# The first token tile runs ahead in both MLPs; low weight halves go into the ring slots; ScalarE casts the input's high halves

## The reference, cut to what matters

```python
h = x
for layer in range(2):                 # layer 0: differential attention, layer 1: block attention
    mix = attention(h)                 # w_in, scores, softmax, w_out
    h = layer_norm(ALPHA * h + mix, ln1_g[layer], ln1_b[layer])
    h = layer_norm(ALPHA * h + square(relu(h @ w_up[layer])) @ w_down[layer], ln2_g[layer], ln2_b[layer])
u = modulate(rmsnorm(h))               # third block: token mixer (retention and latent attention)
h = h + gate * token_mixer(u)          # w_in_2 is 1024 x 6848, and six more matrices
h = h + gate * hier_moe(modulate(rmsnorm(h)))   # 32 experts, 2 per token
out = rmsnorm(h)
```

## Time and profile before

| | us |
|---|---|
| median of three runs | 1192.47 (1191.81 to 1195.05) |
| profiled execution | 1190.7 |
| its span | 1188.9 |
| TensorE busy | 1118.6 (94%) |
| VectorE busy | 699.5 (59%) |
| ScalarE busy | 556.3 (47%) |

### The profile page before, as it was taken

The page is one execution under the profiler, slowest core; times in us unless marked ns, Lnnn a source line. Parts: engine busy times, 40 slices in busy tenths (PEclk is TensorE's granted clock), DMA queues, the critical chain, the costliest instruction groups (busy, mean ns, idle before and its releaser), DMA issues. The chain is left out here.

```text
span 1188.9 us, 17973 instructions
## 1 busy us (share of the span) xinstructions
PE 1118.6 (94%) x7231; PEld 898.8 (76%) x7231; DVE 699.5 (59%) x1041; ACT 556.3 (47%) x953; POOL 52.4 (4%) x94
## 2 busy tenths in 40 slices
PE   7998899999999999999998999999999999889676
PEld 5987688888789987888887878988887866546333
DVE  3487867778766667778778626745456643312112
ACT  4567556556545646555655424345543322213112
POOL 5000000010000000010000000000000000000000
PEclk9999999999999999999998999999999989979988
DMA  9943378888755333888873652455647799999995
GB/s 273 290 168 104 107 224 295 292 280 292 244 163 191 108 117 130 321 293 275 285 262 100 137 177 72 142 206 180 209 139 262 280 374 369 389 398 386 417 416 225
DMA packets 126510, 285.17 MB, mean 240 GB/s; under 512 B 12222, under 2 KB 72891, under 8 KB 118369
## 3 DMA queue, kind: packets, MB, share of 16 engines
q1 hardware_dynamic: 116512, 249.29, 59.9%
q0 software_dynamic: 9920, 34.80, 9.1%
HBM read 281.87 MB, written 2.20 MB: 239 GB/s over the span
## 5 line engine op out<-in xcount | busy, mean ns | idle before, releaser
L2000 DVE TENSOR_TENSOR w_lo<-ring,w_hi 128x1024 fp32r<-128x1024 f32 (+1 forms) x272 | 320.3, 1212 | 101.1 <-ACT w_hi L1507 91.7
L1507 ACT ACTIVATE w_hi<-ring 128x1024 fp32r<-128x1024 f32 (+1 forms) x272 | 277.0, 1047 | 102.8 <-PE acc L680 77.2
L678 PE MATMUL acc<-w_hi,x_two 128*128 128x512 f32 (+2 forms) x320 | 128.5, 402 | 5.3 <-DVE x_two L1985 4.1
L680 PE MATMUL acc<-w_hi,x_two 128*128 128x512 f32 (+2 forms) x320 | 123.4, 386 | 0.0
L679 PE MATMUL acc<-w_lo,x_two 128*128 128x512 f32 (+2 forms) x320 | 123.3, 385 | 0.0
L678 PE MATMUL pp<-x_two,w_hi 128*128 128x256 f32 x384 | 112.5, 293 | 0.0
L679 PE MATMUL pp<-x_two,w_hi 128*128 128x256 f32 x384 | 108.5, 283 | 0.0
L680 PE MATMUL pp<-x_two,w_lo 128*128 128x256 f32 x384 | 108.5, 283 | 0.0
L678 PE MATMUL acc<-w_hi,hid_hi 128*128 128x512 f32 x256 | 99.8, 390 | 0.0
L680 PE MATMUL acc<-w_hi,hid_lo 128*128 128x512 f32 x256 | 99.6, 389 | 0.0
L679 PE MATMUL acc<-w_lo,hid_hi 128*128 128x512 f32 x256 | 99.6, 389 | 0.0
(11 more groups left out here) (397 smaller groups left out, 2135.4 us busy)
## 6 DMA issues: line engine op xcount, KB each, us to landing
ring<-in_w_up_dram SPq DMA_DIRECT2D x32, 1024.0 KB, 5.7
ring<-in_w_down_dram SPq DMA_DIRECT2D x32, 1024.0 KB, 6.6
exp_ring<-in_w_dram SPq DMA_DIRECT2D x32, 1024.0 KB, 11.3
stage<-in_w_ada_dram POOLq DMA_DIRECT2D x48, 512.0 KB, 6.2
ring<-in_w_in_dram SPq DMA_DIRECT2D x24, 1024.0 KB, 5.3
ring<-in_w_in_a_dram SPq DMA_DIRECT2D x12, 1024.0 KB, 14.2
mod<-in_w_dram SPq DMA_DIRECT2D x19, 512.0 KB, 12.9
ring<-in_w_kv_shared_dram SPq DMA_DIRECT2D x8, 1024.0 KB, 6.2
```

Of the source, the lines that this page charges most:

```text
L678: pe.matmul(out, lhs[0], rhs[0], start=start, stop=False)
L680: return pe.matmul(out, lhs[1], rhs[0], start=False, stop=stop)
L1507: act.activation(shaped(high_half(b, k), raw), raw, ACT.Copy).then_inc(S["hi_ready"], 1)
L2000: dve.tensor_tensor(shaped(low_half(b, k), raw), raw, shaped(high_half(b, k), raw), ALU.subtract).then_inc(S["lo_ready"], 1)
```

## The change

1. *Ring and high slots.* `w_lo` goes; `w_hi` has eight halves. For blocks 12 to 99 the low half is written over the raw values in its ring slot, and SP reloads a slot only when TensorE has used the block (`half_used`) instead of when its low half is ready. Other blocks use the upper half of `w_hi` for their lows, as deep as before.
2. *Input.* In all 16 parts ScalarE writes `x_hi` itself, one activation of 128 x 512 behind its four scaled pieces; VectorE only subtracts.
3. *MLP start.* The fillers ahead of each turn go (two remain after the first). Up blocks 0 and 1 run by tile: block 0 on tile 0 (by input halves), the turn of tile 1, block 1 on tile 0, block 0 on tile 1, block 1 on tile 1, then down block 0. Block 0 sums in `acc` banks 0 and 1; the other pairs swap `pp` and `tp`. For one tile the low product has 128 columns and the high product 2 x 128.
4. *MLP end.* Down 14 leaves the second half of tile 1 for later: 18 products, then down 15 on tile 0 (12), then the remaining 6 of down 14 and 12 of down 15.
5. *By tile elsewhere.* `tile_first_out` runs blocks 0 and 1 on tile 0 before tile 1, and the turn of tile 1 stands after block 0's twelve products instead of after six.
6. *Norms.* VectorE normalises tile 0 first, takes the rest of tile 1's sum, and splits parts of tile 0 between; ScalarE casts the first high half of block 1 before the root of tile 1 and the second one after it.
7. *Expert stage.* In the last quad five fillers stand between the w1 product and the wait for w3.

```diff
-HIGHS = 4
+HIGHS = 8
-LOWS = 4
+def in_place(b):
+    return B_ATT[0] + 12 <= b < B_RQK
...
@@ low_half, load
+            if in_place(b):
+                return raw_half(b, k, low_ring)
+            return w_hi[:, HIGHS // 2 + high_slot(b, k), :]
...
+                    if in_place(old):
+                        sp.wait_ge(S["half_used"], half_index(old, 1) + 1)
...
@@ tile_first_out
-                for j in range(4):
-                    if j % 2 == 0:
-                        half_ready(b, j // 2)
-                    part(0, j, 0)
-                    if j == 1:
+                for i in range(2):
+                    for j in range(4):
+                        if j % 2 == 0:
+                            half_ready(b + i, j // 2)
+                        part(i, j, 0)
+                    if i == 0:
                         turn()
                 pe.wait_ge(S["x_split"], base + 3)
-                for j in range(4):
-                    last = part(0, j, 1)
...
@@ TensorE, mlp
+                def up_tile(v, c, k, q):
+                    tok = slice(q * 128, (q + 1) * 128)
+                    sums = up_banks(v)[:, c, :].rearrange("p (a n) -> p a n", a=2)[:, :, tok]
+                    if k == 0 and q == 0:
+                        half_ready(b + v, c)
+                    for kt in range(4 * k, 4 * k + 4):
+                        hi, lo = w_parts(b + v, c, slice(128 * kt, 128 * kt + 128))
+                        if kt:
+                            pe.matmul(sums[:, 0, :], lo, x_hi[:, kt, tok], start=False, stop=False)
+                        last = pe.matmul(sums, hi, x_two[:, :, kt, tok], start=(kt == 0), stop=(kt == KT - 1))
...
+                norm_tile(2 * layer, 0)
+                busy(2)
+                for k in range(2):
+                    pe.wait_ge(S["x_split"], base + 1 + k)
+                    for c in range(2):
+                        up_tile(0, c, k, 0)
+                norm_tile(2 * layer, 1)
+                for c in range(2):
+                    for k in range(2):
+                        up_tile(1, c, k, 0)
+                for k in range(2):
+                    pe.wait_ge(S["x_split"], base + 3 + k)
+                    for c in range(2):
+                        up_tile(0, c, k, 1)
+                for c in range(2):
+                    for k in range(2):
+                        up_tile(1, c, k, 1)
+                down(0)
...
+                for v in range(PAIRS - 2, PAIRS):
+                    pe.wait_ge(S["hid_ready"], PAIRS * layer + v + 1)
+                    for f in range(2):
+                        half_ready(b + min(2 * v + 2, 31), f)
+                    last_parts(v, 0, (0, 1))
+                    if v == PAIRS - 2:
+                        last_parts(v, 1, (0,))
+                last_parts(PAIRS - 2, 1, (1,))
+                last_parts(PAIRS - 1, 1, (0, 1))
...
@@ expert stage, last quad
+                    if s + 1 == QUADS:
+                        busy(5, turn_bank)
...
@@ ScalarE, to_input and norm_input
+                    act.activation(x_hi[:, 4 * half:4 * half + 4, q * 128:(q + 1) * 128], x_f[:, n % 2, :, :],
+                                   ACT.Copy).then_inc(S["xs_high"], 1)
...
                 norm_root(i, 0)
+                scaled(0, 1)
+                high_part(b + 1, 0)
                 norm_root(i, 1)
+                high_part(b + 1, 1)
                 scaled(0, 1)
+                if i != 1:
+                    high(b + 2)
...
@@ VectorE, split_part and layer_norm
-                dve.wait_ge(S["tp_done"], turns_done(g))
+                dve.wait_ge(S["xs_high"], n + 1)
-                link(dve.tensor_copy(x_hi[:, at[0], at[1]], x_f[:, n % 2, :, :]))
...
+                normalise(0)
+                sum_part(i, b, 1, 0)
+                half_sum(i, b, 1, 1)
+                split_input(1)
+                link(half_stats(1, 1))
+                tile_stat(1)
+                split_input(1)
+                normalise(1)
+                low((B_MLP[0], B_ATT[1], B_MLP[1])[i] + 1)
+                split_input(2)
+                if i != 1:
+                    low((B_MLP[0], B_ATT[1], B_MLP[1])[i] + 2)
```

More of the change, by code:

```diff
@@ L689, in w_parts @@
             def w_parts(b, k, cols):
-                return high_half(b, k)[:, cols], low_half(b, k)[:, cols]
+                low = low_half(b, k)
+                if len(low.shape) == 3:
+                    assert cols.stop - cols.start == 128
+                    return high_half(b, k)[:, cols], low[:, cols.start // 128, :]
+                return high_half(b, k)[:, cols], low[:, cols]
             def arrive(b):
@@ L975, in mlp @@
                 inputs[0] += 4
-                def before(j):
-                    if j < 2:
-                        pe.wait_ge(S["x_split"], base + 3 + j)
                 def up(v):
[L983 to L986, removed]
+                    pe.wait_ge(S["sum_done"], PAIRS * layer + v - 1)
+                    pairs_out(b + 2 * v - 1, up_banks(v))
+                def up_tile(v, c, k, q):
[8 more added lines that the diff above has]
+                        last = pe.matmul(sums, hi, x_two[:, :, kt, tok], start=(kt == 0), stop=(kt == KT - 1))
+                        if kt == 0:
+                            pe.matmul(sums[:, 0, :], lo, x_hi[:, kt, tok], start=False, stop=False)
+                    if k == 1 and q == 1:
+                        last.then_inc(S["half_used"], 1)
                 def down_part(v, j, q):
@@ L1007, in mlp @@
+                for k in range(2):
[6 more added lines that the diff above has]
+                down(0)
+                for v in range(1, PAIRS - 2):
                     up(v + 1)
-                    if v == 0:
-                        pe.wait_ge(S["ln_stat"], 4 * layer + 2)
@@ L1010, in mlp, with last_parts @@
                     down(v)
[L1011 to L1015, removed]
+                up(PAIRS - 1)
+                def last_parts(v, q, halves):
+                    for half in halves:
                         for f in range(2):
-                            last = down_part(PAIRS - 1, 2 * f + half, q)
+                            last = down_part(v, 2 * f + half, q)
@@ L1671, in mlp @@
                         .then_inc(S["rest_ready"], 1)
-                    high(b + 2 * v + 2 - (v > 0) if v < PAIRS - 1 else b + 31)
+                    if v:
+                        high(b + 2 * v + 1)
                     act.wait_ge(S["sum_done"], j + 1)
@@ L1956, in _ @@
             inputs = [0]
-            input_groups = [g + i for g in SHIFTED_AT for i in range(4)]
             plain = [0]
@@ L1996, in low_part @@
                 dve.wait_ge(S["hi_ready"], x + 1)
-                if x >= LOWS:
-                    dve.wait_ge(S["half_used"], x - LOWS + 1)
+                if x >= HIGHS // 2 and not in_place(b):
+                    dve.wait_ge(S["half_used"], x - HIGHS // 2 + 1)
                 raw = raw_half(b, k)
```

87 lines of the change are left out of this document (39 added, 48 removed).

## The result

The changed kernel takes 1202.27 us (median of 18 runs, 1192.34 to 1207.35), the kernel before 1188.01 us in 18 runs on the same chip (1181.80 to 1195.05). The ratio is 1.0113, 95% interval 1.0094 to 1.0132: 13.4 us slower. The forecast was 1196.0, range 1190 to 1209. The direction was right and the range held it; the forecast is 6.3 us short.

The account below looks back on a forecast made before the run. TensorE, busy 94% of the span, was taken as the bound, the change being decided at its breaks. +1.8 - 1.3 + 5.7 - 2.65 = +3.6 us on 1190.7 gives 1194.3; with 1.8 for the median, 1196.0, range 1190 to 1209.

Parts of the forecast that it names:

- Input and MLP start: At both MLP starts, the first down product comes 0.9 us later with a pair at 0.23 us: +1.8 in all.
- End of the MLPs: Ahead of the last down block TensorE idles 1.2 us; price and gain both about zero.
- The second norm: At the norm of i = 1, block 2 starts at 339.1 instead of 340.40: -1.3 us.
- Norm ahead of the third block: TensorE idles 5.6 us awaiting block 97's halves, then runs at low clock: +5.7 us, ends 3.55 and 7.
- What follows: Behind the third block's start, loads of blocks 100 to 105 and latents shift by the same as the products.
- Ring and depth: Loads waiting for TensorE's use of a block instead of its low half make nothing wait; worth nothing.
- Last quad: Five fillers in a 4.9 us wait keep 2.4 GHz; the 64 products cost 3.7 instead of 6.35 us: -2.65.
- small products dear: Rival at MLP starts: small products cost more than columns and load, pair up to 0.347, 1209.5 us; chance 0.17.
- the clock holding: Rival ahead of the third block: no low clock behind the idle stretch, 2.1 us less, 1194; chance 0.12.

Follow-up runs that it names:

- g1_wide: The changed kernel with each low product of an MLP's first two half blocks taking 256 columns instead of 128: 1201.6 us, ratio 1.0121.
- e3_ring: The changed kernel with low halves in ring slots only up to block 95, so loads 100 to 103 wait for low halves again: 1197.3 us, ratio 1.0085.
- f1_late: The changed kernel with block 105's halves cast behind the latents' copies and first four query projections (VectorE: their rotations): 1191.7 us, ratio 1.0037.
- e1_early: The changed kernel with block 97's high and low halves cast ahead of the second tile's input, not behind the whole input: 1195.1 us, ratio 1.0052.
- g2_noplace: The changed kernel with block 97's halves early and 105's late, but no low halves in ring slots and four high halves: 1201.8 us, ratio 1.0121.
- f4_before_busy: The kernel before with only the last quad's five fillers added: 1185.0 us, ratio 0.9970.
- g3_again: The changed kernel without any edit, run and profiled a second time: 1201.7 us, ratio 1.0109 against the kernel before.
- g4_before_late: The kernel before with the last quad's five fillers and block 105's halves cast late: 1184.7 us, ratio 0.9975.
- e4_both: The changed kernel with block 97's halves early and the old ring rule from block 96 on: 1190.3 us, ratio 1.0010.

## Why the prediction was right in sign and short in size

- *Input and MLP start* (+0.9 each, a pair at 0.23): right. 0.23 measured, 21.76 against 20.74 us, +1.0. g1_wide shows that columns don't set the price, as the prediction said; that the load of the weights does, it leaves likely but not shown. By the 81 ns of the Trainium skill (TensorE: Matmul & The Clock Gate, Back-to-back issue gap) a pair at 0.20 would have come out, an estimate from that figure and the 0.12 of a 256-column product. The trace doesn't agree for these products: 0.11 is left for the one of 128 columns, and the measurement decides.
- *End of the MLPs* (1.2 us idle, price nothing): right, 1.08 idle; the next norm's first product is no later.
- *The second norm* (first product 326.56, block 2 at 339.1): 326.57 and 339.16.
- *Norm ahead of the third block* (5.6 us idle to 652.1, low clock behind it, +5.7 at block 98): 5.55, to 652.17, at 0.50; +5.6.
- "What follows (loads of blocks 100 to 105, latents) waits for the same products and shifts by the same": **this step failed**. It is the one sentence of that part without a row. Block 98 is 5.6 us late, the latents' first product 10.3, the next attention 11.2. It treated the loads as tied to the products already; before, they were tied to the low halves, which ran ahead of the products. The first projection load stood 1.6 us *ahead* of block 98's start (652.67 against 654.25); in after it goes out 4.0 us *behind* it (663.90 against 659.86), since it waits for its end. The new order lets 5.6 us pass, the new ring rule adds 5.6, and the slack that 105's cast had in before (0.50 us) didn't cover it. How far the rule is at fault, e3_ring shows: with the old rule and the new order the 4.86 us are 0.63. f1_late takes the second loss away alone, 6.4 us of the third block, e1_early the first, 6.5; together 14.2.
- *Ring and depth* ("nothing waits"; a wait could only show inside an MLP): right in the MLPs, wrong in the third block, the same gap in the argument: the loads there aren't of the MLP's kind, and nine issues follow each other. What the rule and the depth are good for was not seen either: without both the new order costs 17 us more (g2_noplace).
- *Last quad* (-2.65): right, -3.6 with an interval of 1.3 to 5.9 (f4_before_busy), -3.2 in the last quad of after; the products take 3.6 us in place of 6.3.

The sum: forecast +3.6. The terms that it has, as measured, give the same: 1.2, 5.6 and -3.2. What is missing is the term that it put at nothing, 5.6 us more in the third block. With it, it is +1.2 for the layers up to 621 us (+1.0 at the first MLP's start; in the first profile of after 1.2 us of chance in the first attention hide it: one stretch there, 103.55 to 117.20, takes 13.65 us, and 14.87 in before and in g3_again), +11.2 for the third block, -3.2 for the last quad: +9.2. The medians, against which the chance in one profile doesn't count, say +13.4, 11.2 to 15.7 by the interval. Some 4 us are therefore not placed (2 to 6.5). They may be a matter of how often the fall of the clock told below happens: the mean granted clock of after's executions has a median of 0.969, that of its profiled one is 0.972. No run shows it.

None of the rivals was this one. The nearest rules, small products dear and the clock holding, are both refuted (0.23; 0.50). That the range held the result is luck: its upper end, 1209, came from small products being dear.

## What to carry to other kernels

When a buffer's release moves from "converted" to "used", list every load behind it in the queue up to the last one that any engine waits for in its program order, and look at how early each went out before: here nine issues of 11.7 us stood between the release and the load that mattered, and the slack behind it was 0.50 us. A cast of a late block placed ahead of short urgent copies is a trap that costs nothing until the load is late; moved behind them it gave 6.4 us of the third block here and nothing where the load was early. And an idle stretch ahead of a block is best removed where the waiting engine has a hole: 97's two casts fit in ScalarE's wait for tile 1, and both moves together beat both kernels (1184.8 against 1188.2). But the kernel before with the fillers alone does as well (1185.0), so that all the rest of the change, mended, is worth nothing that these runs can tell.

## What was not expected of the hardware

Some 220 us behind the third attention's transposes, in the router's products, the clock falls with TensorE busy all along. It does so in most profiles, not in all; the same 20 us there in before and in g4_before_late:

```profile
947.12:967.12 20.00, 19.54 (x134) 13.95 (x136) 13.61 (x51) 5.97 (x13) 1.66 (x4) 0.74 1.00 407
```

```profile
945.43:965.43 20.00, 18.23 (x190) 12.73 (x191) 14.86 (x54) 6.12 (x13) 1.67 (x4) 1.00 1.01 416
```

The three profiles in which it is 1.00 (e3_ring, e4_both, g4_before_late) take 453.3 to 455.5 us from those transposes to the end, the others 457.5 to 463.2. In f1_late and f4_before_busy the same 20 us stand at 0.91 and 0.93, in the rest at 0.70 to 0.74. It doesn't follow the order of the products: one of the three has that of before, two that of after. What sets it off is open. So a single profile of this kernel is uncertain by some 5 us or more behind 940 us, and the comparison of milestones ahead of that point says more than its span.

A product of 128 columns behind one of 256 begins 0.06 us ahead of the next, and that one 0.17 ahead of its follower: the pair, not the single row, has the price.
